# An expert stage whose rows are gathered and transposed once for two experts

## The chip, the cores and the metric

One core of a Trainium2 chip runs the whole kernel. The metric is the device time in microseconds, the median of the runs.

## The reference

One encoder layer over 512 tokens of width 2048: a mixer (two kinds of attention, gated and added to the residual) gives h, and a mixture of experts is added to it. What matters here is the second half:

```
hn = rms_norm(h, norm2_g)                       # h * r[token] * g[column]
group = argmax(hn @ w_rg + b_rg); top 2 of its 8 experts by hn @ w_re + b_re
weight = p_group * softmax(top 2)
for each expert e of 32, its tokens as rows:
    y = (silu(rows @ w_gate[e]) * (rows @ w_up[e])) @ w_down[e] * weight
    out[token] = h[token] + sum of its two y
```

silu(a) is a * sigmoid(a). Gate and up are 2048 x 512, down is 512 x 2048, float32: 12 MB an expert. There are 1024 pairs of token and expert.

## The kernel before, in words

The first half (to about 1256 us) computes h in float32 out of products of high and low parts, writes h also to a DRAM copy, h_dram, and sums the squares for the root-mean-square factor r of each token. A routing part on VectorE then makes tables with a column for each item of work and a row for each of an item's slots: `idx_x` (the token in the slot, out of bounds if it is empty), and `tab` with three fields, token, weight and r (lines 983 to 985).

An item is one expert with at most 64 tokens (SLOTS). With these inputs there are 32 items. Each engine loops over pairs of items, an even and an odd one, and the engines keep in step by semaphores alone. For an item:

- POOL gathers the rows of h_dram into `xg`, 64 x 2048, by one indirect DMA (L528 for the first, L537 in the loop). It first copies the item's column of indices (L533) and waits until TensorE has transposed the rows before. Empty slots move no row.
- ScalarE multiplies `xg` by r of each slot (`rows_scaled`, L848).
- TensorE transposes it in 16 pieces (`x_transpose`, L1612) into PSUM banks 2 and 3. VectorE copies them, times g, to `xT` (`x_copy`, L1228).
- TensorE multiplies `xT` with gate into bank 0 and with up into bank 1, 128 matmuls in four groups (L1637), one for each quarter of the weights. Half f of the columns goes to partitions 64 f and on.
- ScalarE makes the sigmoid of bank 0 (`sg`, L856), VectorE two products (`t1`, `hs`, L1258 and L1259), TensorE transposes `hs` (L1650), VectorE copies it (`hT`, L1263), TensorE multiplies by down in four groups (L1663).
- ScalarE (`y_hi`, L861) and VectorE (`y_lo`, L1275) scale by the weight and split the result into two parts. Even and odd item use different halves of the partitions. VectorE makes `place`, which has a one where the slot's token is (L1271).
- TensorE adds both items of the pair before to their tokens by `combine` (L1622), two of its eight steps after each group of the even item's gate and up, into banks 2, 3 (even steps) and 6, 7 (odd ones). VectorE adds each to `h` (`add_parts`, L1237).

The order on TensorE is written by hand: the transposes for the next item stand between the up matmuls and the down matmuls; in the even item behind the transposes of hs and a wait for the seventh add, in the odd one ahead of them.

SP issues every load of weights (`item_loads`, L446), quarters of 1 MB, in the order of use. Gate has two buffers, up and down have one, all in quarters: up and gate of the next items are loaded into a quarter as soon as a group of L1637 has used it (L403, L399), down as soon as a group of L1663 has (L406). The four buffers are filled before the first item begins, and SP then waits for its first group. Behind the last loads SP waits for the adds and writes `h` out.

Two more lines stand in the rows: L1551 transposes h for the router in pieces of 128 x 128, and L134 is a wait.

Of the kernel before, what the change touches and what calls it, by code (L numbers as in the profile page):

```python
# [27 lines left out]
F32 = mybir.dt.float32  # L28
F32R = mybir.dt.float32r
U32 = mybir.dt.uint32  # L30
# [38 lines left out]
ITEMS = EXPERTS + XTRA + 1  # L69
# [59 lines left out]
def build(nc, x, norm1_g, w_in, q_norm_a, k_norm_a, sink_a, q_norm_b, k_norm_b, rpb_pad, w_up_a, w_up_b,  # L129
# [4 lines left out]
    with ctx:  # L134
# [19 lines left out]
        xg = sb("xg", [SLOTS, D], F32, R0 + 32 * K)  # L154
        xT = sb("xT", [P, KT, SLOTS], F32, R0 + 40 * K)

        y_hi = [sb(f"y_hi{f}", [P, D // 2], F32R, (R0 + 44 * K, R3 + 32 * K)[f]) for f in range(2)]
        y_lo = [sb(f"y_lo{f}", [P, D // 2], F32R, (R0 + 48 * K, R4 + 1536)[f]) for f in range(2)]
        place = [sb(f"place{f}", [P, S], F32R, (R0 + 56 * K, R3 + 36 * K)[f]) for f in range(2)]
        sg = sb("sg", [P, F // 2], F32, R0 + 52 * K)  # L160
        t1 = sb("t1", [P, F // 2], F32, R0 + 53 * K)
        hs = sb("hs", [P, F // 2], F32, R0 + 54 * K)
        hT = sb("hT", [P, 2, P], F32, R0 + 55 * K)
        token = sb("token", [P, S], F32, R0 + 62 * K)
        tab = sb("tab", [P, 3, ITEMS], F32, R0 + 60 * K)
        idx_x = sb("idx_x", [SLOTS, ITEMS], U32, R0 + 61 * K)
        cur_x = sb("cur_x", [SLOTS, 1], U32, R0 + 61 * K + 256)
        cur = sb("cur", [P, 2], F32, R0 + 61 * K + 288)
# [68 lines left out]
        for name, shape in (("L", [P, NT, LOG]), ("gm", [P, 4]), ("gd", [P, 4, 4]), ("eg", [P, 4, 4]),  # L237
# [46 lines left out]
        (s_gu, s_dn, s_gath, s_xs, s_xt2, s_xTc, s_sgm, s_hs, s_hst, s_hTc, s_yhi, s_ylo, s_comb, s_added, s_nreg) = (  # L284
            sem(n) for n in ("s_gu", "s_dn", "s_gath", "s_xs", "s_xt2", "s_xTc", "s_sgm", "s_hs", "s_hst", "s_hTc", "s_yhi",
# [198 lines left out]
        def _(pool):  # L484
# [35 lines left out]
            items = pool.value_load(nitem[0:1, 0:1], min_val=EXPERTS, max_val=EXPERTS + XTRA)  # L520
# [9 lines left out]
            with pool.Fori(0, items) as i:  # L530

                pool.wait_ge(s_gath, i * 16 + 16)
                nc.gpsimd.tensor_copy(cur_x[:], idx_x[:, ds(i + 1, 1)]).then_inc(s_pool, 1)  # L533
                pool.wait_ge(s_pool, i + 2)
                pool.wait_ge(s_xt2, i + 1)
                settle(pool, s_pool_passed)
                gp.indirect_dma_start(xg[:], None, h_d, bass.IndirectOffsetOnAxis(ap=cur_x[:, 0:1], axis=0),  # L537
                                      bounds_check=S - 1, oob_is_err=False).then_inc(s_gath, 16)
# [21 lines left out]
        def _(act):  # L560
# [304 lines left out]
        def routing(dve, own, V):  # L865
# [117 lines left out]
            own.do(ts(idx_x[:], tab_ps[0:SLOTS, 0, :], 2.0 * S, None, ALU.add))  # L983
# [11 lines left out]
        def _(dve):  # L995
# [228 lines left out]
            g2b = bc(g2m[:], SLOTS)  # L1224
# [25 lines left out]
            with dve.Fori(0, pairs) as p:  # L1250
                own.loop(p, 0, 4)
                for odd in range(2):
                    i = p * 2 + odd
                    if not odd:
                        add_parts(p, range(6))

                    dve.wait_ge(s_sgm, i + 1)
                    own.do(V.tensor_tensor(t1[:], sg[:], PS[:, 0, 0:F // 2], ALU.mult))  # L1258
                    V.tensor_tensor(hs[:], t1[:], PS[:, 1, 0:F // 2], ALU.mult).then_inc(s_hs, 1)  # L1259
# [6 lines left out]
                    x_copy(i + 1)  # L1266

                    own.do(V.tensor_copy(cur[:], tab[:, 0:2, ds(i, 1)].rearrange("p c o -> p (c o)")))
                    for f in range(2):
                        q = slice(SLOTS * (f ^ odd), SLOTS * (f ^ odd) + SLOTS)  # L1270
                        V.tensor_scalar(place[f][q, :], token[q, :], cur[q, 0:1], None, ALU.is_equal)  # L1271
                    dve.wait_ge(s_yhi, i + 1)
                    for f in range(2):
                        q = slice(SLOTS * (f ^ odd), SLOTS * (f ^ odd) + SLOTS)
                        last = V.scalar_tensor_tensor(out=y_lo[f][q, :], in0=PS[q, 4:6, :].rearrange("p a b -> p (a b)"),  # L1275
                                                      scalar=cur[q, 1:2], in1=y_hi[f][q, :].bitcast(F32),
# [6 lines left out]
        def _(pe):  # L1283
# [457 lines left out]
```

## Time and profile before

| | us |
|---|---|
| median of 3 runs | 2326.51 |
| lowest and highest | 2323.01, 2326.81 |
| span of the profiled execution, first to last instruction | 2323.9 |
| expert stage in it, from the first gate matmul (1302.9) to the end | 1021.0 |
| busy in the span: TensorE, VectorE, ScalarE, GpSimd | 2165.1, 851.9, 650.2, 67.4 |

The page gives the profiled execution by its span; a time of the device for the same execution is not in it. The median of the runs is 2.6 us above this span. Busy TensorE means that a matmul is under way, not that it is at its peak. DMA busy share is that of the core's 16 DMA engines. The granted clock is 1.0 at TensorE's 2.4 GHz and 0.5 at 1.2 GHz.

### The profile page before, as it was taken

The page shows a single profiled execution, that of the slowest core. Times are in us where ns is not written, and L with a number is a line of the kernel's source. Part 1 is how long each engine was busy: PE and PEld are TensorE (multiplying, and loading weights), DVE is VectorE, ACT ScalarE, POOL GpSimd, SP SyncE. Part 2 cuts the span into 40 slices and gives each one's busy share as a digit, 9 for nine tenths or more (in the row PEclk, how much of TensorE's full clock was granted, in tenths as well). Part 3 has the DMA queues.
Part 4 walks back from the last instruction along what each step waited for, and adds up shares of the span by engine and source line. Part 5 has one row for each costly group of instructions (what it writes and reads, how often), then busy time and mean ns, then how long its engine had stood idle before and what let it go on. Part 6 is the DMA issues. An engine that isn't in the chain of part 4 may idle for free.

```text
span 2323.9 us, 31259 instructions
## 1 busy us (share of the span) xinstructions
PE 2165.1 (93%) x12178; PEld 1583.7 (68%) x12178; DVE 851.9 (37%) x1131; ACT 650.2 (28%) x816; POOL 67.4 (3%) x114
## 2 busy tenths in 40 slices
PE   5999999999999999999997699989988989888887
PEld 4888888888888888888886455555555555555554
DVE  4555454544222222224223433333333233333324
ACT  4446455453222222223322122212122112121121
POOL 1000000010000000000000000000000000000000
PEclk9999999999999999999998799999999999999998
DMA  5422222322333333336544599999999999999994
GB/s 178 124 82 77 86 88 76 95 78 86 95 99 96 94 99 97 92 99 195 198 147 162 195 410 408 407 415 411 408 407 399 405 410 414 405 397 410 415 388 179
DMA packets 264062, 541.99 MB, mean 233 GB/s; under 512 B 24856, under 2 KB 200152, under 8 KB 212696
## 3 DMA queue, kind: packets, MB, share of 16 engines
q1 hardware_dynamic: 260776, 532.57, 61.6%
q0 software_dynamic: 3248, 8.90, 1.4%
q8 instruction: 25, 0.41, 0.1%
q14 instruction: 13, 0.11, 0.0%
HBM read 541.93 MB, written 11.55 MB: 238 GB/s over the span
## 4 chain that ended last, share of the span: by engine, by line
PE 76%; DMA 15%; DVE 4%; issue 2%; ACT 1%; ACTq 0%; SPq 0%; DVEq 0%; POOL 0%; POOLq 0%
DMA wd_s<-in_w_down 14%; PE PS L1307 13%; PE PS L1309 13%; PE PS L1308 13%; PE PS L1637 10%; PE PS L1663 7%; PE PS L1622 5%; PE PS L1324 3%; PE PS L1326 3%; PE PS L1325 3%; PE PS L1612 2%; PE PS L1380 1%; DVE h L1237 1%; DVE y_lo L1275 1%; ACT y_hi L861 1%
## 5 line engine op out<-in xcount | busy, mean ns | idle before, releaser
L1019 DVE TENSOR_TENSOR w_lo<-w_raw,w_hi 128x1024 fp32r<-128x1024 f32 x200 | 245.0, 1225 | 673.0 <-ACT w_hi L585 673.0
L1307 PE MATMUL PS<-x_hi,w_hi 128*128 128x512 f32 x1088 | 431.2, 396 | 2.4 <-DVE x_lo L1012 2.4
L1309 PE MATMUL PS<-x_hi,w_lo 128*128 128x512 f32 x1088 | 424.6, 390 | 0.0
L1308 PE MATMUL PS<-x_lo,w_hi 128*128 128x512 f32 x1088 | 424.3, 390 | 0.0
L585 ACT ACTIVATE w_hi<-w_raw 128x1024 fp32r<-128x1024 f32 x200 | 211.8, 1059 | 703.6 <-PE PS L1309 574.9
L1637 PE MATMUL PS<-wu_s,xT 128*64 128x256 f32 x2048 | 312.4, 381 | 0.0
L1663 PE MATMUL PS<-wd_s,hT 128*64 128x512 f32 x1024 | 245.8, 631 | 33.5 <-DMA wd_s<-in_w_down 25.2
L1307 PEld LDWEIGHTS PS<-x_hi,w_hi 128*128 128x128 f32 x1088 | 204.6, 188 | 46.7 <-issue 3.0
L1308 PEld LDWEIGHTS PS<-x_lo,w_hi 128*128 128x128 f32 x1088 | 204.8, 188 | 43.5 <-issue 2.4
L1309 PEld LDWEIGHTS PS<-x_hi,w_lo 128*128 128x128 f32 x1088 | 204.6, 188 | 43.5
L1237 DVE TENSOR_TENSOR h<-h,PS 128x1024 f32<-128x1024 f32 x136 | 161.3, 1217 | 136.2 <-PE PS L1622 135.8
L1637 PEld LDWEIGHTS PS<-wu_s,xT 128*64 128x64 f32 x2048 | 153.9, 138 | 69.8 <-issue 2.6
L1663 PEld LDWEIGHTS PS<-wd_s,hT 128*64 128x64 f32 x1024 | 72.6, 142 | 178.8 <-issue 126.1
L1637 PE MATMUL PS<-wg_odd,xT 128*64 128x256 f32 x1024 | 157.4, 381 | 27.9 <-DMA wu_s<-in_w_up 27.9
L1275 DVE SCALAR_TENSOR_TENSOR y_lo<-PS,cur,y_hi 64x1024 fp32r<-64x1024 f32 x64 | 82.1, 1283 | 274.0 <-ACT y_hi L861 273.5
L861 ACT ACTIVATE y_hi<-PS,tab 64x1024 fp32r<-64x1024 f32 x64 | 71.0, 1110 | 382.8 <-PE PS L1663 382.4
L1637 PE MATMUL PS<-wg_s,xT 128*64 128x256 f32 x1024 | 160.2, 392 | 4.6 <-DMA wu_s<-in_w_up 3.0
L856 ACT ACTIVATE sg<-PS 128x256 f32<-128x256 f32 x32 | 12.3, 384 | 422.6 <-PE PS L1637 422.6
L1637 PEld LDWEIGHTS PS<-wg_odd,xT 128*64 128x64 f32 x1024 | 76.4, 137 | 74.2 <-issue 47.5
L1622 PE MATMUL PS<-y_hi,place 128*128 128x512 f32 x272 | 93.1, 424 | 24.0 <-DVE y_lo L1275 23.5
L1637 PEld LDWEIGHTS PS<-wg_s,xT 128*64 128x64 f32 x1024 | 69.9, 139 | 64.4 <-issue 25.0
L1324 PE MATMUL PS<-w_hi,m_hi 128*128 128x512 f32 x256 | 101.4, 396 | 2.8 <-DVE h L1200 2.8
(222 smaller groups left out, 2314.5 us busy)
## 6 DMA issues: line engine op xcount, KB each, us to landing
wu_s<-in_w_up SPq DMA_DIRECT2D x128, 1024.0 KB, 25.6
wd_s<-in_w_down SPq DMA_DIRECT2D x128, 1024.0 KB, 25.2
w_raw<-in_w_in SPq DMA_DIRECT2D x136, 512.0 KB, 3.8
wg_s<-in_w_gate SPq DMA_DIRECT2D x64, 1024.0 KB, 26.7
wg_odd<-in_w_gate SPq DMA_DIRECT2D x64, 1024.0 KB, 28.5
w_raw<-in_w_out SPq DMA_DIRECT2D x32, 512.0 KB, 3.9
w_raw<-in_w_up_a SPq DMA_DIRECT2D x16, 512.0 KB, 3.9
w_raw<-in_w_up_b SPq DMA_DIRECT2D x16, 512.0 KB, 3.9
```

The source lines that it names most:

```text
L585: act_fn(w_hi[:, b, :], w_raw[:, r, :], ACT.Copy).then_inc(s_whi, 1)
L861: last = act_fn(y_hi[f][q, :], PS[q, 4:6, :].rearrange("p a b -> p (a b)"), ACT.Copy, scale=tab[q, 1, ds(i, 1)])
L1019: V.tensor_tensor(w_lo[:, b, :], w_raw[:, r, :], w_hi[:, b, :].bitcast(F32), ALU.subtract).then_inc(s_wlo, 1)
L1237: V.tensor_tensor(hv, hv, PS[:, bank:bank + 2, :], ALU.add).then_inc(s_added, 1)
L1275: last = V.scalar_tensor_tensor(out=y_lo[f][q, :], in0=PS[q, 4:6, :].rearrange("p a b -> p (a b)"), scalar=cur[q, 1:2], in1=y_hi[f][q, :]. ...
L1307: mm(PS[:, bank, :], wh[:, k, :], rhs_hi[:, k0 + k, :], start=(start and k == 0), stop=False)
L1308: mm(PS[:, bank, :], wh[:, k, :], rhs_lo[:, k0 + k, :], start=False, stop=False)
L1309: last = mm(PS[:, bank, :], wl[:, k, :], rhs_hi[:, k0 + k, :], start=False, stop=(stop and k == 7))
L1324: mm(o, a_hi, b_hi, start=start, stop=False)
L1622: last = mm(PS[:, bank + f, :], place[f][:, t * P:t * P + P], y[f][:, m * S:m * S + S], start=(y is y_hi), stop=(y is y_lo))
L1637: last = mm(PS[SLOTS * f:SLOTS * f + SLOTS, bank, 0:F // 2], xT[:, k, :], w[:, k, f * (F // 2):(f + 1) * (F // 2)], start=(k == 0), stop=( ...
L1663: last = mm(PS[q:q + SLOTS, 4 + m, :], hT[:, cc, SLOTS * j:SLOTS * j + SLOTS], wd_s[:, c, f * (D // 2) + m * S:f * (D // 2) + m * S + S], ...
```

## The change

Rows are gathered once for a pair: `xg` has 128 partitions, 64 for each item, `idx_x` holds a column of indices for each pair, and POOL, x_transpose and x_copy go once a pair. The transposes are of 128 x 128 and fill banks 2, 3, 6 and 7, and x_copy takes two instructions. The transposes for the next pair stand in the odd item alone, at their former place there, behind a wait for all eight adds of the pair. The factor r is no longer applied to `xg`: sigmoid gets it as a scale, and the two products multiply by it. `cur`, the item's three fields, is copied ahead of them.

```diff
-ITEMS = EXPERTS + XTRA + 1
+ITEMS = EXPERTS + XTRA + 2
+PAIRS = ITEMS // 2
-        xg = sb("xg", [SLOTS, D], F32, R0 + 32 * K)
-        xT = sb("xT", [P, KT, SLOTS], F32, R0 + 40 * K)
+        xg = sb("xg", [P, D], F32, R0 + 32 * K)
+        xT = sb("xT", [P, KT, P], F32, R0 + 40 * K)
...
-        idx_x = sb("idx_x", [SLOTS, ITEMS], U32, R0 + 61 * K)
-        cur_x = sb("cur_x", [SLOTS, 1], U32, R0 + 61 * K + 256)
-        cur = sb("cur", [P, 2], F32, R0 + 61 * K + 288)
+        idx_x = sb("idx_x", [P, PAIRS], U32, R0 + 61 * K)
+        cur_x = sb("cur_x", [P, 1], U32, R0 + 61 * K + 256)
+        cur = sb("cur", [P, 2, 3], F32, R0 + 61 * K + 288)
...
@@ POOL @@
-            with pool.Fori(0, items) as i:
-                pool.wait_ge(s_gath, i * 16 + 16)
-                nc.gpsimd.tensor_copy(cur_x[:], idx_x[:, ds(i + 1, 1)]).then_inc(s_pool, 1)
-                pool.wait_ge(s_pool, i + 2)
-                pool.wait_ge(s_xt2, i + 1)
+            with pool.Fori(0, pairs) as p:
+                pool.wait_ge(s_gath, p * 16 + 16)
+                nc.gpsimd.tensor_copy(cur_x[:], idx_x[:, ds(p + 1, 1)]).then_inc(s_pool, 1)
+                pool.wait_ge(s_pool, p + 2)
+                pool.wait_ge(s_xt2, p + 1)
...
@@ ScalarE @@
-            def rows_scaled(i):
-                act.wait_ge(s_gath, i * 16 + 16)
-                act_fn(xg[:], xg[:], ACT.Copy, scale=tab[0:SLOTS, 2, ds(i, 1)]).then_inc(s_xs, 1)
-            rows_scaled(0)
...
-                    rows_scaled(i + 1)
                     act.wait_ge(s_gu, i * 4 + 4)
-                    act_fn(sg[:], PS[:, 0, 0:F // 2], ACT.Sigmoid).then_inc(s_sgm, 1)
+                    act_fn(hs[:], PS[:, 0, 0:F // 2], ACT.Sigmoid, scale=tab[:, 2, ds(i, 1)]).then_inc(s_sgm, 1)
...
@@ VectorE @@
-            own.do(ts(idx_x[:], tab_ps[0:SLOTS, 0, :], 2.0 * S, None, ALU.add))
+            by_pair = tab_ps[:, 0, :].rearrange("q (i o) -> q i o", o=2)
+            for o in range(2):
+                own.link(ts(idx_x[SLOTS * o:SLOTS * o + SLOTS, :], by_pair[SLOTS * o:SLOTS * o + SLOTS, :, o], 2.0 * S, None, ALU.add))
...
-            def x_copy(i):
-                dve.wait_ge(s_xt2, i + 1)
-                V.tensor_tensor(xT[:], PS[:, 2:4, :].rearrange("p a (k s) -> p (a k) s", s=SLOTS), g2b,
-                                ALU.mult).then_inc(s_xTc, 1)
+            def x_copy(p):
+                dve.wait_ge(s_xt2, p + 1)
+                for half, bank in enumerate((2, 6)):
+                    last = V.tensor_tensor(xT[:, 8 * half:8 * half + 8, :],
+                                           PS[:, bank:bank + 2, :].rearrange("p a (k s) -> p (a k) s", s=P),
+                                           g2b[:, 8 * half:8 * half + 8, :], ALU.mult)
+                last.then_inc(s_xTc, 1)
...
+                    own.do(V.tensor_copy(cur[:, odd, :], tab[:, :, ds(i, 1)].rearrange("p c o -> p (c o)")))
                     if not odd:
                         add_parts(p, range(6))
                     dve.wait_ge(s_sgm, i + 1)
-                    own.do(V.tensor_tensor(t1[:], sg[:], PS[:, 0, 0:F // 2], ALU.mult))
-                    V.tensor_tensor(hs[:], t1[:], PS[:, 1, 0:F // 2], ALU.mult).then_inc(s_hs, 1)
+                    own.do(V.scalar_tensor_tensor(out=hs[:], in0=PS[:, 0, 0:F // 2], scalar=cur[:, odd, 2:3], in1=hs[:],
+                                                  op0=ALU.mult, op1=ALU.mult))
+                    V.scalar_tensor_tensor(out=hs[:], in0=PS[:, 1, 0:F // 2], scalar=cur[:, odd, 2:3], in1=hs[:],
+                                           op0=ALU.mult, op1=ALU.mult).then_inc(s_hs, 1)
...
-                    x_copy(i + 1)
-                    own.do(V.tensor_copy(cur[:], tab[:, 0:2, ds(i, 1)].rearrange("p c o -> p (c o)")))
+                    if odd:
+                        x_copy(p + 1)
...
@@ TensorE @@
-            def x_transpose(i):
-                pe.wait_ge(s_xs, i + 1)
+            def x_transpose(p):
+                pe.wait_ge(s_gath, p * 16 + 16)
...
-                    o = PS[:, 2 + k // 8, (k % 8) * SLOTS:(k % 8) * SLOTS + SLOTS]
-                    last = nc.tensor.transpose(o, v[:, k, :], mats[0:SLOTS, 0, 0:SLOTS])
+                    o = PS[:, (2, 3, 6, 7)[k // 4], (k % 4) * P:(k % 4) * P + P]
+                    last = nc.tensor.transpose(o, v[:, k, :], ident)
...
-                pe.wait_ge(s_xTc, i + 1)
+                if not odd:
+                    pe.wait_ge(s_xTc, p + 1)
...
-                                last = mm(PS[SLOTS * f:SLOTS * f + SLOTS, bank, 0:F // 2], xT[:, k, :],
+                                last = mm(PS[SLOTS * f:SLOTS * f + SLOTS, bank, 0:F // 2], xT[:, k, SLOTS * odd:SLOTS * odd + SLOTS],
...
                 if odd:
-                    pe.wait_ge(s_added, p * 8 + 9)
-                    x_transpose(i + 1)
+                    pe.wait_ge(s_added, p * 8 + 10)
+                    x_transpose(p + 1)
                 pe.wait_ge(s_hs, i + 1)
...
-                if not odd:
-                    pe.wait_ge(s_added, p * 8 + 9)
-                    x_transpose(i + 1)
                 pe.wait_ge(s_hTc, i + 1)
```

## Rows read from the trace of the kernel before

**Rows 1.** The page's strip of 40 slices of 58 us: what the core's DMA moved
```profile
...
GB/s 178 124 82 77 86 88 76 95 78 86 95 99 96 94 99 97 92 99 195 198 147 162 195 410 408 407 415 411 408 407 399 405 410 414 405 397 410 415 388 179
...
```

**Rows 2.** Table by stretch: busy us (instructions), granted clock, DMA busy share, GB/s
```profile
...
1306.00:1308.00 2.00, 2.00 (x16) 1.23 (x14) 0.00 (x0) 1.14 (x1) 0.18 (x1) 0.65 0.02 8
1332.00:1334.00 2.00, 2.00 (x12) 0.72 (x10) 0.87 (x2) 0.00 (x0) 0.16 (x1) 1.00 0.81 238
1500.00:1700.00 200.00, 183.59 (x1243) 106.58 (x1242) 69.24 (x85) 37.52 (x32) 7.96 (x14) 0.97 1.01 409
...
```

**Rows 3.** Chain of waits, expert stage: start us, us, what
```profile
...
1302.92 5.88 PE PS L1637 x32
...
1310.83 3.60 PE PS L1637 x32
...
1364.86 1.29 DVE y_lo L1275
...
1422.42 1.29 DVE y_lo L1275
...
1543.01 1.29 DVE y_lo L1275
...
2211.89 28.77 DMA wd_s<-in_w_down
...
2246.35 1.29 DVE y_lo L1275
...
```

**Rows 4.** DMA traffic in 12 us: 1896 to 1908, 1884 to 1896, 1782 to 1794
```profile
...
DMA packets 696, 5.08 MB, mean 423 GB/s; under 512 B 76, under 2 KB 76, under 8 KB 76
...
DMA packets 711, 4.74 MB, mean 395 GB/s; under 512 B 132, under 2 KB 132, under 8 KB 132
...
q0 software_dynamic: 80, 0.16, 4.5%
...
GB/s 437 382 437 437 437 437 410 410 410 410 410 437 410 437 382 218 191 218 164 300 137 300 246 273 218 273 191 410 355 410 437 410 437 410 410 437 437 437 437 437
DMA packets 612, 4.34 MB, mean 362 GB/s; under 512 B 82, under 2 KB 82, under 8 KB 82
...
q0 software_dynamic: 80, 0.43, 14.6%
...
```

**Rows 5.** Timeline of the head: start us, us, engine, instruction [idle before <-releaser]
```profile
...
1293.02 1.01 POOL L528 DMA_INDIRECT xg<-h_dram,cur_x  x1 [0.85 <-POOL cur_x L526]
...
1297.24 2.00 ACT L848 ACTIVATE xg<-xg,tab 64x2048 f32<-64x2048 f32 x1 [22.12 <-DMA xg<-h_dram,cur_x]
...
1299.34 2.01 PE L1612 MATMUL PS<-mats,xg 64*128 64x64 f32 x16 [8.83 <-ACT xg L848]
1301.46 1.23 DVE L1228 TENSOR_TENSOR xT<-PS,g2m 128x1024 f32<-128x1024 f32 x1 [4.17 <-PE PS L1612]
...
```

**Rows 6.** Timeline of TensorE: transposes of line 1551
```profile
...
1257.31 1.09 PE L1551 MATMUL PS<-mats,h 128*128 128x128 f32 x8 [2.65 <-DVE h L1200]
...
1263.01 1.09 PE L1551 MATMUL PS<-mats,h 128*128 128x128 f32 x4
...
```

**Rows 7.** Timeline of the last pair of items
```profile
...
2254.62 2.35 DVE L1237 TENSOR_TENSOR h<-h,PS 128x1024 f32<-128x1024 f32 x2 [3.29 <-PE PS L1622]
...
2267.13 0.42 DVE L1263 COPY hT<-PS 128x256 f32<-128x256 f32 x1
...
2267.45 1.94 PE L1612 MATMUL PS<-mats,xg 64*128 64x64 f32 x16 [0.44 <-DVE h L1237]
...
2269.33 7.09 PE L1663 MATMUL PS<-wd_s,hT 128*64 128x512 f32 x32
...
2292.60 0.42 DVE L1263 COPY hT<-PS 128x256 f32<-128x256 f32 x1 [1.04 <-PE PS L1650]
...
2293.08 0.20 PEld L1663 LDWEIGHTS PS<-wd_s,hT 128*64 128x64 f32 x4 [0.71 <-DVE hT L1263]
...
```

**Rows 8.** Transfers of wd_s issued from 2240 to 2246 us
```profile
...
DMA to landing us min/median/max: 27.2/27.5/27.7
...
```

More of the change, by code:

```diff
@@ L153, in build @@
         wd_s = sb("wd_s", [P, 4, D], F32, R0)
-        xg = sb("xg", [SLOTS, D], F32, R0 + 32 * K)
-        xT = sb("xT", [P, KT, SLOTS], F32, R0 + 40 * K)
[L157 to L163, printed above, removed]
+        xg = sb("xg", [P, D], F32, R0 + 32 * K)
+        xT = sb("xT", [P, KT, P], F32, R0 + 40 * K)
+        y_hi = [sb(f"y_hi{f}", [P, D // 2], F32R, (R0 + 48 * K, R3 + 32 * K)[f]) for f in range(2)]
+        y_lo = [sb(f"y_lo{f}", [P, D // 2], F32R, (R0 + 52 * K, R4 + 1536)[f]) for f in range(2)]
+        place = [sb(f"place{f}", [P, S], F32R, (R0 + 58 * K, R3 + 36 * K)[f]) for f in range(2)]
+        hs = sb("hs", [P, F // 2], F32, R0 + 56 * K)
+        hT = sb("hT", [P, 2, P], F32, R0 + 57 * K)
         token = sb("token", [P, S], F32, R0 + 62 * K)
         tab = sb("tab", [P, 3, ITEMS], F32, R0 + 60 * K)
-        idx_x = sb("idx_x", [SLOTS, ITEMS], U32, R0 + 61 * K)
-        cur_x = sb("cur_x", [SLOTS, 1], U32, R0 + 61 * K + 256)
-        cur = sb("cur", [P, 2], F32, R0 + 61 * K + 288)
+        idx_x = sb("idx_x", [P, PAIRS], U32, R0 + 61 * K)
+        cur_x = sb("cur_x", [P, 1], U32, R0 + 61 * K + 256)
+        cur = sb("cur", [P, 2, 3], F32, R0 + 61 * K + 288)
         eid = sb("eid", [P, XTRA], I32, R0 + 61 * K + 320)
@@ L283, in build @@
         s_wd = [sem(f"s_wd{c}") for c in range(4)]
-        (s_gu, s_dn, s_gath, s_xs, s_xt2, s_xTc, s_sgm, s_hs, s_hst, s_hTc, s_yhi, s_ylo, s_comb, s_added, s_nreg) = (
-            sem(n) for n in ("s_gu", "s_dn", "s_gath", "s_xs", "s_xt2", "s_xTc", "s_sgm", "s_hs", "s_hst", "s_hTc", "s_yhi",
+        (s_gu, s_dn, s_gath, s_xt2, s_xTc, s_sgm, s_hs, s_hst, s_hTc, s_yhi, s_ylo, s_comb, s_added, s_nreg) = (
+            sem(n) for n in ("s_gu", "s_dn", "s_gath", "s_xt2", "s_xTc", "s_sgm", "s_hs", "s_hst", "s_hTc", "s_yhi",
                              "s_ylo", "s_comb", "s_added", "s_nreg"))
@@ L519, in _ @@
             pool.wait_ge(s_r1, 1)
-            items = pool.value_load(nitem[0:1, 0:1], min_val=EXPERTS, max_val=EXPERTS + XTRA)
+            pairs = pool.value_load(nitem[0:1, 2:3], min_val=EXPERTS // 2, max_val=(EXPERTS + XTRA) // 2)
             pool.wait_ge(s_hd, 16 * NT)
@@ L1223, in _ @@
             pairs = dve.value_load(nitem[0:1, 2:3], min_val=EXPERTS // 2, max_val=(EXPERTS + XTRA) // 2)
-            g2b = bc(g2m[:], SLOTS)
-            def x_copy(i):
-                dve.wait_ge(s_xt2, i + 1)
-                V.tensor_tensor(xT[:], PS[:, 2:4, :].rearrange("p a (k s) -> p (a k) s", s=SLOTS), g2b,
-                                ALU.mult).then_inc(s_xTc, 1)
+            g2b = bc(g2m[:], P)
+            def x_copy(p):
[5 more added lines that the diff above has]
+                last.then_inc(s_xTc, 1)
             def add_parts(p, parts):
@@ L1265, in _ @@
                         add_parts(p, (7,))
-                    x_copy(i + 1)
-                    own.do(V.tensor_copy(cur[:], tab[:, 0:2, ds(i, 1)].rearrange("p c o -> p (c o)")))
+                    if odd:
+                        x_copy(p + 1)
                     for f in range(2):
                         q = slice(SLOTS * (f ^ odd), SLOTS * (f ^ odd) + SLOTS)
-                        V.tensor_scalar(place[f][q, :], token[q, :], cur[q, 0:1], None, ALU.is_equal)
+                        V.tensor_scalar(place[f][q, :], token[q, :], cur[q, odd, 0:1], None, ALU.is_equal)
                     dve.wait_ge(s_yhi, i + 1)
@@ L1275, in _ @@
                         last = V.scalar_tensor_tensor(out=y_lo[f][q, :], in0=PS[q, 4:6, :].rearrange("p a b -> p (a b)"),
-                                                      scalar=cur[q, 1:2], in1=y_hi[f][q, :].bitcast(F32),
+                                                      scalar=cur[q, odd, 1:2], in1=y_hi[f][q, :].bitcast(F32),
                                                       op0=ALU.mult, op1=ALU.subtract)
```

## The prediction

> **What bounds the kernel now.** I read the 40-slice strip of the page first. From the 24th slice on, where the experts run, the core moves about 408 GB/s in every slice but the last two, against 77 to 198 before [rows 1]. The table by stretch says how full that is: from 1500 to 1700 us the DMA engines are 1.01 busy at 409 GB/s while TensorE is busy 183.59 of 200 us [rows 2]. So the expert stage is a stream of weights, 32 experts of 12 MB. The chain of waits agrees and adds a history [rows 3]. The low halves of the result (y_lo) of even items follow each other by 1422.42 - 1364.86 = 57.6 us while TensorE still works on weights that came early; from 1543.01 to 2246.35 there are 11 pairs of items, 63.9 us each, and each such pair has a wait on a transfer of wd_s in the chain, such as the 28.77 us from 2211.89. A pair of items that TensorE could do in 57.6 us takes the 63.9 us that its weights need. Engine time removed in the middle of the stage therefore buys nothing. The change can act in three places: on the stream itself, before the stream is full, and after the last weights.
>
> **The stream.** What disturbs it are the gathers of xg. In 12 us without one, 5.08 MB move (423 GB/s). In 12 us around a gather that brings 0.16 MB (19 rows of 8 KB) it is 4.74 MB, around one that brings 0.43 MB (53 rows) 4.34 MB, gathered bytes included [rows 4]. So these losses come on top of the gathered bytes. The first loses 0.34 MB = 0.80 us of stream, the second 0.74 MB = 1.75 us. A straight line through both gives 0.0118 MB, 0.028 us, for each row and a remainder of 0.12 MB, 0.28 us, for a gather as such. Both gathers have 80 packets, 64 slots and 16 more, so an empty slot is part of that remainder. The change makes 17 gathers of 128 slots out of 33 of 64, with the same 1024 rows. Per-row loss stays. If slots make the remainder, it stays too; if the gather as such does, half of it goes. Bounds: 0 and 0.28 us. I take 0.15, the middle, since nothing in the rows separates them. Some 15 of the 16 dropped gathers lie in the full stream: 15 x 0.15 = **-2.2 us** (0 to -4.2). The gather of a pair may land later than now; it is issued right after the transposes of the pair before, so some 50 of the 63.9 us cover it.
>
> **Removed, and worth nothing by itself.** Scaling xg on ScalarE, 2.00 us 33 times [rows 5], runs while TensorE is in its matmuls, except for the first one. Every second x_transpose, x_copy and index copy of POOL goes; the tile sg becomes hs, and the factor moves into the sigmoid's scale and the two products, which keep their count and size (0.42 us each). The copy of cur moves ahead of the products; 0.16 us, behind which only adds wait whose matmuls come later. POOL's wait for a gather, then for the transpose, now happens once a pair; nobody stands behind it. x_transpose in the odd item now waits for all eight adds of the pair, made a whole item earlier. SP's queue issues what it did, in the same order.
>
> **Before the stream is full: the head.** Now: the gather is issued at 1293.02, ScalarE starts at 1297.24, the transposes at 1299.34, the copy at 1301.46, the matmuls at 1302.92 [rows 5]. After:
> - two index operations for one, 50 columns for 49 in the routing tables: +0.2.
> - the gather of 64 + 64 slots: 4.2 us from issue to use for 64 slots. Between +0 (all latency) and +4.2 (all proportional); +1.2, nearer to latency, since the dent that 53 rows make in the stream spans only 12 or 13 slices of 0.3 us, 3.8 us [rows 4].
> - no scaling: from 1297.24 to 1299.34, -2.1.
> - 16 transposes of 128 x 128 instead of 64 x 128. This is a low-clock stretch (clock 0.65 from 1306 to 1308, and the first group of 32 matmuls of L1637 takes 5.88 us against 3.60 later) [rows 2, 3]. Transposes of 128 x 128 in L1551 took 1.09 us for 8 before the clock fell and 1.09 for 4 after it [rows 6]. So 16 of them take about 2.1 us at the high level and 3.7 at the low one; now 2.01. I take +1.7 (0 to +1.7).
> - two copies of 128 x 1024: two such operations run in 2.35 us [rows 7], one in 1.23: +1.1.
>
> Sum +2.1. The first group starts later but spends less of itself at the low clock, up to 1.1 us back if the clock rises when it does now; I count +1.6 (-1 to +5). The transfers wait for that group, so the stream starts 1.6 later. Against it stands the first even item: its x_transpose (1.94 us between the last gate and up matmul and the first of the down matmuls) is gone, so wd_s comes free relatively earlier. Now there is a hole: 238 GB/s from 1332 to 1334 [rows 2], 0.9 us of stream. It closes: -0.9. **Head: +0.7.**
>
> **After the last weights: the tail.** From 2246.35 on the chain is TensorE's without a wait on weights. In the last even item hT's copy starts at 2267.13 but the down matmuls at 2269.33, behind the transposes; in the odd item, where nothing stands between, they start 0.48 after that copy (2292.60 to 2293.08) [rows 7]. So the even item's down matmuls start at 2267.6: -1.7. The weights just allow it: wd_s took up to 27.7 us to land [rows 8], so the last quarter, issued before 2245, is there by 2272.7, and would be wanted 5.3 us after the start, at 2272.9. In the odd item the transposes of 128 slots stand between gate/up and the down matmuls; at the high clock 16 take 2.1 us by L1551 against 1.94 to 2.01 now: +0.1 (up to +1.7 at the low level's price). hs is ready under them. The doubled x_copy stands ahead of y_lo on VectorE, 1.1 us longer, but y_lo has to wait for ScalarE anyway, which waits for down matmuls of 7.09 us [rows 7]. **Tail: -1.6.**
>
> **Sum.** -2.2 + 0.7 - 1.6 = -3.1 us on a span of 2323.9. The median of the runs shown, 2326.5, is 2.6 above that span; with the same distance I forecast 2323.4, 0.13% less. About 0.2%, 4.7 us, is what a measurement of this kernel can tell from no change, so the forecast is: no difference that counts.
>
> **Rivals.**
> A, faster: the loss belongs to the gather, not to its rows, because the packets of one gather run in one batch on each DMA engine. Then 15 gathers less save up to their mean loss, (0.80 + 1.75)/2 = 1.3 us each: -19, or about 2306 with the other terms. Against it: 53 rows cost more than twice what 19 do [rows 4]. For it: no row shows a gather of 128 slots.
> The Trainium skill, page DMA: Bandwidth & Descriptors, section Anatomy of one DMA, speaks for more: about 2.0 us fixed for each DMA from GpSimd. If that were stream time, 15 gathers less would give -30 us. The trace disagrees: the smallest gather shown costs 0.80 us in all, so most of any fixed part is latency beside a busy stream.
>
> B, slower: the slots that hold tokens fall on fewer DMA engines. They are the first ones of each 64. If 128 slots are dealt so that those land on eight engines, each of these carries 64 rows more than an even share. One of sixteen engines moves 423/16 = 26.4 GB/s, so a row costs its engine 0.0082 MB/26.4 = 0.31 us for its bytes and 16 x 0.028 = 0.45 beyond them. 64 x 0.76 = 49 us, and the stream ends with its slowest engine: about 2372, less by what the rows are uneven already. It decides in the middle of the stage, as soon as rates between gathers fall below 423.
> The Trainium skill, same page, section The descriptor swizzle, says engines 0 to 7 write partitions 0 to 63 and 8 to 15 the others, four partitions each in turn; by that the first 32 slots of both halves spread over all sixteen, and B would not happen. No row here names an engine.
>
> C, slower at both ends: the first gather's time is proportional (+3 beyond my term), the clock stays low a little longer (+2), transposes cost 3.7 in the tail too (+1.6), the fixed gather cost stays (+2.2). About 2332.
>
> **Chances.** Forecast case 0.70, A 0.15, B 0.06, C 0.09. The forecast case's own range is 2318 to 2329; some of it, and A, lie more than 0.2% below 2326.5: 0.30 faster. B and most of C: 0.13 slower. The rest, 0.57, within. The range for 8 in 10 takes the forecast case whole, the near part of A and half of C: 2313 to 2332.
>
> **What would show it.** In the profile after: between 1500 and 2200 the pair of items again at 63.5 to 64 us and the DMA engines at 1.0; TensorE's idle before wd_s larger by about 1.7 us a pair; a dent of 1.5 to 2.9 us of stream for each of 16 gathers, in place of two of half that; first matmul of L1637's line at about 1305 instead of 1302.92; from the last even y_lo to the end about 1.6 us less than 2323.9 - 2246.35 = 77.6. A pair under 63 us would make A right; a rate between gathers under 420 GB/s would make B right; a first matmul after 1307, C. The forecast is wrong if the median leaves 2313 to 2332.

## The result, and the profile after

| | before | after |
|---|---|---|
| median of 4 runs each, us | 2325.8 (2323.01 to 2326.81) | 2291.02 (2288.81 to 2292.28) |
| ratio, 95% interval | | 0.9853 [0.9842, 0.9865] |
| profiled execution, us | span 2323.9 | time 2290.01, span 2288.1 |

The change takes 34.8 us away. I had forecast 3.1, with a range that ended at 2313 below. The mechanism that pays is one that I had priced and then assumed to stay.

The strip of the page comes first again (40 slices, now of 57 us), then the table by stretch, with columns as in [rows 2].

```profile
...
GB/s 179 121 89 79 78 89 86 81 87 83 94 99 95 98 95 97 96 96 195 197 120 92 208 392 421 421 422 421 422 422 421 422 422 421 422 422 422 421 420 208
...
```

```profile
...
1328.00:1330.00 2.00, 1.23 (x6) 0.67 (x4) 0.84 (x2) 1.07 (x2) 0.00 (x0) 1.00 0.89 291
1334.00:1336.00 2.00, 2.00 (x13) 0.59 (x10) 0.00 (x0) 0.00 (x0) 0.00 (x0) 1.00 0.71 176
1500.00:1700.00 200.00, 181.47 (x1260) 103.89 (x1258) 71.62 (x88) 23.99 (x25) 3.61 (x6) 1.00 1.01 422
...
```

Where [rows 1] has 397 to 415 GB/s from the 24th slice to the 38th, the 25th to the 39th now hold 420 to 422. The DMA engines are 1.01 busy in both tables, at 409 GB/s in [rows 2] and at 422 here: they were as busy and moved less. TensorE is busy 181.47 of the 200 us (183.59 before) although the stage goes faster: it now makes 16 transposes of xg for a pair instead of 32.

The chain of waits of the expert stage (start us, us, what) gives the landmarks that [rows 3] gave.

```profile
...
1303.68 6.58 PE PS L1638 x32
...
1366.10 1.29 DVE y_lo L1275
...
1423.44 1.29 DVE y_lo L1275
...
1539.67 1.29 DVE y_lo L1275
...
2212.41 1.29 DVE y_lo L1275
...
2230.96 1.28 ACT L848
2235.28 7.09 PE PS L1661 x32
...
2258.94 7.11 PE PS L1661 x32
...
```

Set against [rows 3], three distances account for the whole. The first even y_lo stands at 1366.10, 1.24 later than 1364.86. From there to the last even y_lo it is 2212.41 - 1366.10 = 846.3 us against 881.5: 35.2 less. From that y_lo to the end it is 2288.1 - 2212.41 = 75.7 against 77.6: 1.9 less. 1.2 - 35.2 - 1.9 = -35.9, the difference of the spans (35.8) but for rounding. The 11 pairs from 1539.67 to 2212.41 take 61.2 us each; they took 63.9. The pair that TensorE paces is what it was: 1423.44 - 1366.10 = 57.3 against 57.6. So the head and the tail came out near the forecast, and the stream, where I counted 2.2 us, gave all the rest.

What a gather costs the stream is read from the DMA traffic. First the 12 us from 1710 to 1722, around a gather of 0.74 MB, 90 rows; then the traffic of the same 11 pairs in both kernels: before from 1543.01 to 2246.35, after from 1539.67 to 2212.41.

```profile
...
DMA packets 736, 5.06 MB, mean 422 GB/s; under 512 B 118, under 2 KB 118, under 8 KB 118
...
q0 software_dynamic: 144, 0.74, 15.0%
...
```

```profile
...
GB/s 420 403 417 410 422 402 398 421 397 421 397 421 390 392 410 422 388 400 423 404 422 399 422 397 394 421 423 394 381 422 381 423 405 422 397 398 422 401 392 401
DMA packets 40222, 286.13 MB, mean 407 GB/s; under 512 B 5296, under 2 KB 5296, under 8 KB 5296
...
q0 software_dynamic: 1760, 6.06, 3.2%
...
```

```profile
...
GB/s 422 421 422 420 421 424 420 422 422 421 421 421 422 421 421 422 424 421 421 421 422 421 421 421 422 422 422 421 422 421 421 422 421 422 422 422 421 421 421 420
DMA packets 39751, 283.64 MB, mean 422 GB/s; under 512 B 5130, under 2 KB 5130, under 8 KB 5130
...
q0 software_dynamic: 1584, 5.70, 2.1%
...
```

In [rows 4], 53 rows left 4.34 MB of the 5.08 that 12 us can hold. Now 90 rows leave 5.06. Over the 11 pairs of before, 286.13 MB would take 678.0 us at 422 GB/s; they took 703.3, so 25.3 us were lost beyond the bytes, for 6.06 MB, 740 rows. After, 283.64 MB need 672.1 of 672.7 us: 0.6 us lost, for 696 rows. The rows are still moved. Only their surcharge is gone. This quantity, **the time beyond the bytes at 422 GB/s**, is the measure of all that follows. The 422 is itself the rate of after, to three digits, so a loss of 1 or 2 us in 700 is not told from none. Counted from the first even y_lo on, with the three pairs ahead of the 11 (73.00 and 73.15 MB), before loses 30.5 us and after 0.8: that is 29.6 of the 35.2 us. The other 5.5 are 2.34 MB that the change moves outside this stretch and before moves within it.

### The profile page after: what moved, and what is told of

It is laid out like the page before. It is cut to its first block, busy times and chain, and to the rows that moved or that the text cites. A ratio compares the mean times of both kernels' runs of the same rounds, so it can differ in the third digit from the quotient of the medians.

```text
span 2288.1 us, 30507 instructions
## 1 busy us (share of the span) xinstructions
PE 2121.8 (93%) x11922; PEld 1547.4 (68%) x11922; DVE 853.2 (37%) x1133; ACT 566.3 (25%) x767; POOL 50.3 (2%) x82
## 4 chain that ended last, share of the span: by engine, by line
PE 78%; DMA 13%; DVE 4%; issue 2%; ACT 2%; ACTq 0%; SPq 0%; DVEq 0%; POOL 0%; POOLq 0%
PE PS L1307 13%; PE PS L1309 13%; PE PS L1308 13%; PE PS L1638 12%; DMA wd_s<-in_w_down 8%; PE PS L1661 7%; PE PS L1622 5%; DMA wu_s<-in_w_up 4%; PE PS L1324 3%; PE PS L1326 3%; PE PS L1325 3%; PE PS L1380 1%; ACT L848 1%; PE PS L1558 1%; DVE y_lo L1275 1%
## 5 line engine op out<-in xcount | busy, mean ns | idle before, releaser
L1661 PE MATMUL PS<-wd_s,hT 128*64 128x512 f32 x1024 | 230.8, 600 | 41.8 <-DVE hT L1263 23.5
```

The lines of the kernel that those rows point to most:

```text
L1661: last = mm(PS[q:q + SLOTS, 4 + m, :], hT[:, cc, SLOTS * j:SLOTS * j + SLOTS], wd_s[:, c, f * (D // 2) + m * S:f * (D // 2) + m * S + S], ...
```

## The experiments

The diff changes several things about a gather at once: how many there are, how many slots each has, and on which partitions of xg they land. The kernels pull these apart. e1 to e4 ran on one chip beside 19 runs of before (2324.6 us), e5 to e8 on one with 7 (2325.71), e9 and e10 with 7 (2326.23).

**e1: 33 gathers of 128 slots, the upper 64 always empty.** From before: xg, xT's source, idx_x and cur_x get 128 partitions. All rows still land on partitions 0 to 63.

```diff
-        xg = sb("xg", [SLOTS, D], F32, R0 + 32 * K)
+        xg = sb("xg", [P, D], F32, R0 + 32 * K)
...
-            own.do(ts(idx_x[:], tab_ps[0:SLOTS, 0, :], 2.0 * S, None, ALU.add))
+            own.link(ts(idx_x[0:SLOTS, :], tab_ps[0:SLOTS, 0, :], 2.0 * S, None, ALU.add))
+            own.do(ts(idx_x[SLOTS:P, :], tab_ps[SLOTS:P, 0, :], 0.0, 2.0 * S, ALU.mult, ALU.add))
```

> The kernel before, with one thing changed: xg and its indices have 128 partitions and the upper 64 slots are always empty, so the 33 gathers, their rows and everything else stay. Theory 1 (a row costs stream time beyond its bytes because the gather is written for 64 partitions): the stream runs at 421 to 423 GB/s through every gather, a pair of items takes 61.2 us instead of 63.9, and the time is about 2325.8 - 32 x 1.05 = 2292; if the rows now fall on eight of the sixteen DMA engines, up to 20 us more than that. Theory 2 (the loss is one of each gather, and the change gained because it has 17 for 33): 33 dents of about 1 us as before, 2326. Theory 3 (scaling xg in place disturbs the stream): also 2326.

**e3: the same 33 gathers of 128 slots, but items take the halves in turn.** Even items fill slots 0 to 63, odd ones 64 to 127, and the other half is empty. Scaling and transposes follow the half.

```diff
+            for o in range(2):
+                q = slice(SLOTS * o, SLOTS * o + SLOTS)
+                own.link(ts(idx_x[q, o::2], tab_ps[q, 0, o::2], 2.0 * S, None, ALU.add))
+                own.link(ts(idx_x[q, 1 - o::2], tab_ps[q, 0, 1 - o::2], 0.0, 2.0 * S, ALU.mult, ALU.add))
...
-                act_fn(xg[:], xg[:], ACT.Copy, scale=tab[0:SLOTS, 2, ds(i, 1)]).then_inc(s_xs, 1)
+                act_fn(xg[q, :], xg[q, :], ACT.Copy, scale=tab[q, 2, ds(i, 1)]).then_inc(s_xs, 1)
```

> The kernel before, with 128 slots in each of the 33 gathers, of which even items fill the lower 64 and odd items the upper 64; scaling and transposes work on that half. Same rows, same number of gathers. Theory 1: no dents, 421 to 423 GB/s all through, 2292, and 2291 to 2294 whatever the lower-half kernel gives, since both groups of engines get rows. Theory 2: 2326. Theory 3: 2326.

Measured: e3 2292.68 us, ratio 0.9864 [0.9847, 0.9880]; e1 2315.26, 0.9956 [0.9939, 0.9972]. Traffic of the 11 pairs of e3 (1537.81 to 2214.49):

```profile
...
DMA packets 41465, 284.94 MB, mean 421 GB/s; under 512 B 6686, under 2 KB 6686, under 8 KB 6686
...
q0 software_dynamic: 3168, 6.06, 2.4%
...
```

284.94 MB need 675.2 of 676.7 us: 1.5 us lost in 22 gathers, with the same 740 rows for which before lost 25.3. **e3 keeps before's number of gathers, its scaling, its transposes and its copies, and has the gain of the change**, 31.9 us against its own before where the change has 34.8; the intervals of 0.9864 and 0.9853 overlap. What pays is neither fewer gathers nor less work on any engine; it is that the gather spans 128 partitions instead of 64. The rows themselves still land on 64 partitions, the lower or the upper ones by turns; the other 64 slots of each gather are empty. Doubling the slots cost nothing that can be seen: 3168 packets on the gather's queue instead of 1760.

e1 has the same wide gather and 22.6 us more. Its strip, and the 12 us from 1943 to 1955 around a gather of 0.32 MB (39 rows):

```profile
...
GB/s 172 125 88 78 81 93 76 88 87 82 99 92 100 96 95 100 93 97 196 191 143 143 201 407 421 421 421 421 421 421 409 409 408 409 402 401 406 418 382 173
...
```

```profile
...
DMA  9999999975575395699999999999999989578999
...
DMA packets 700, 4.33 MB, mean 361 GB/s; under 512 B 172, under 2 KB 172, under 8 KB 172
...
q0 software_dynamic: 144, 0.32, 8.1%
...
```

Up to about 1740 us the slices hold 421 like e3's; from there they fall to 401 to 418. In the 12 us some slices have the engines busy 3 to 7 tenths only, and 0.75 MB less goes through than the 5.08 that fit. That is what rival B described: rows that all fall on part of the engines, which fall behind by their extra bytes until the weights wait for them. B's own numbers fit. 64 of the 128 rows on such an engine are above an even share, and 64 x 0.31 us = 19.8 us of bytes; measured 22.6. The 0.45 us a row beyond the bytes that I had added to it was not there, although all rows land on the same partitions 0 to 63 as in before. The trace shows the lag itself. It keeps 16 completion marks for each weight transfer, as many as there are DMA engines. Over the transfers of up and down, the first and the last of the 16 lie 3.7 us apart in e1 (median) between 1350 and 1450 us and 19.9 us apart between 1750 and 1850; in e3 it is 2.8 and 9.4. The Trainium skill, page DMA: Bandwidth & Descriptors, section The descriptor swizzle, has engines 0 to 7 write partitions 0 to 63 of a 128-partition transfer and 8 to 15 the others; e1 and e3 agree with that by 22.6 us, though no row names an engine.

**e2: the change with two gathers of 64 partitions for each pair**, one into partitions 0 to 63, one into 64 to 127.

```diff
-                gp.indirect_dma_start(xg[:], None, h_d, bass.IndirectOffsetOnAxis(ap=cur_x[:, 0:1], axis=0),
+                gp.indirect_dma_start(xg[0:SLOTS, :], None, h_d, bass.IndirectOffsetOnAxis(ap=cur_x[:, 0:1], axis=0),
                                       bounds_check=S - 1, oob_is_err=False).then_inc(s_gath, 16)
+                gp.indirect_dma_start(xg[SLOTS:P, :], None, h_d, bass.IndirectOffsetOnAxis(ap=cur_x[:, 1:2], axis=0),
+                                      bounds_check=S - 1, oob_is_err=False).then_inc(s_gath, 16)
```

> The changed kernel, with the 128 slots of a pair filled by two gathers of 64 partitions each, one right behind the other, into the lower and the upper half of xg. Theory 1: the whole loss is back, 0.03 us a row, 2291 + 32 x 1.05 = about 2325. Theory 2, counted by gathers: about 2325 as well; counted by times at which gathers disturb the stream (16 as in the changed kernel): 2291 to 2308. Theory 3 (scaling xg in place): stays at 2291.

Measured: 2328.9 us, ratio 1.0018 [1.0008, 1.0028]. The pair takes 64.1 us. Traffic of its 11 pairs (1546.37 to 2251.23):

```profile
...
GB/s 422 422 422 374 422 422 369 422 423 421 348 423 422 409 366 424 422 367 423 422 421 351 423 421 406 351 423 422 355 421 422 423 361 421 420 410 364 422 414 420
DMA packets 40211, 285.71 MB, mean 405 GB/s; under 512 B 5337, under 2 KB 5337, under 8 KB 5337
...
```

285.71 MB need 677.0 of 704.9 us: 27.8 lost. Everything of the change is in this kernel but the width of the gather, and the gain is gone, with 0.2% more. For 696 rows 27.8 us are 0.040 us a row, more than before's 0.034; why isn't known. The slices show it by eye: 422, and 348 to 374 where a double gather stands. Using both halves of the partitions by turns doesn't help; each transfer has to span all 128.

**e4: the factor moved alone.** The scaling of xg goes, as in the change; gathers, transposes and copies stay per item.

```diff
-            rows_scaled(0)
...
-                    rows_scaled(i + 1)
...
-                    act_fn(sg[:], PS[:, 0, 0:F // 2], ACT.Sigmoid).then_inc(s_sgm, 1)
+                    act_fn(sg[:], PS[:, 0, 0:F // 2], ACT.Sigmoid, scale=tab[:, 2, ds(i, 1)]).then_inc(s_sgm, 1)
...
-                    own.do(V.tensor_tensor(t1[:], sg[:], PS[:, 0, 0:F // 2], ALU.mult))
+                    own.do(V.scalar_tensor_tensor(out=t1[:], in0=PS[:, 0, 0:F // 2], scalar=cur[:, odd, 2:3], in1=sg[:], op0=ALU.mult, op1=ALU.mult))
...
```

> The kernel before, with the root-mean-square factor moved to the sigmoid's scale and the two products, and no scaling of xg on ScalarE; items are gathered and transposed one by one as before. Theories 1 and 2: the stream keeps its dents, and only the head gets shorter by the first scaling, about 2 us; less up to 1.3 us where a table load of ScalarE comes into the chain of the last even item: 2323 to 2326. Theory 3: the dents go, about 2291.

Measured: 2328.8 us, ratio 1.0022 [1.0012, 1.0031]: 4.2 us slower, though the first group of gate and up matmuls lets its first transfer go 4.7 us earlier than before's. Table by stretch and timeline of e4:

```profile
...
1320.00:1340.00 20.00, 18.24 (x98) 9.07 (x96) 6.17 (x9) 3.97 (x4) 1.13 (x2) 0.83 0.81 293
...
```

```profile
...
1321.17 1.28 ACT L849 ACT_TABLE_LOAD   x1 [47.14 <-PE PS L1630]
...
1322.47 0.47 ACT L849 ACTIVATE sg<-PS,tab 128x256 f32<-128x256 f32 x1
...
```

And ScalarE's timeline of before, for the same even item:

```profile
...
1310.19 1.28 ACT L856 ACT_TABLE_LOAD   x1
1325.76 0.39 ACT L856 ACTIVATE sg<-PS 128x256 f32<-128x256 f32 x1 [14.29 <-PE PS L1637]
...
```

Before, the same 20 us held 363 GB/s at a clock of 1.00 and 19.56 us of TensorE; here 293 at 0.83 and 18.24. (363 - 293) x 20 / 422 = 3.3 us of stream go there. The timeline shows what stands in it: the sigmoid is preceded by a load of ScalarE's function table, 1.28 us. Before, that load followed the scaling at 1310.19 and was long done when the sigmoid's wait ended at 1325.76. With the scaling gone the sigmoid is the first activation after y_hi, the load stands behind the wait, and in the even item TensorE has nothing to do in that time. In the last even item the same load is followed by a down group of 8.69 us at low clock. Why the clock fell isn't shown: the change has the same load in its first even item, at 1327.32, and its clock stays at 1.00 from 1320 to 1340 us. 11 pairs of e4 lose 26.0 us, as before's do. Against before's trace, e4's first even y_lo is 0.4 us earlier, the way from there to the last one is 0.7 longer, and from that one to the end 1.5, in which the load is 1.28. These make 1.8 us; the rest of the 4.2 between the medians is in no trace. The time is above the 2323 to 2326 expected.

**e5 and e6: the disputed cost by itself.** In both, each item's rows are replaced by a plain transfer of the first 64 rows of h (the routing's choice of rows is left out), so the gathered bytes are the same for every item: e5 into 64 partitions, e6 into 128, each row in two halves. 33 x 64 = 2112 rows each, no index read, every slot full.

```diff
e5
+                gp.dma_start(xg[:], h_d[0:SLOTS, :]).then_inc(s_gath, 16)
e6
+                gp.dma_start(xg[:, 0:D // 2], h_d[0:SLOTS, :].rearrange("s (o c) -> (s o) c", o=2)).then_inc(s_gath, 16)
```

> The kernel before, with each of the 33 gathers replaced by a plain transfer from the same queue of GpSimd, rows 0 to 63 of h into the 64 partitions of xg (so the right rows are no longer fetched, and 64 rows come instead of 32 on average). 1088 more rows are 8.9 MB, 21 us of stream. If any transfer into 64 partitions loses 0.032 us a row: 2325 + 21 + 1088 x 0.032 = 2381. If only indirect ones do: 2292 + 21 = 2313.

> The same plain transfer of 64 rows, but as 128 half rows of 4 KB into 128 partitions (the other half of xg stays zero, so the values are not the rows). Same bytes as in the plain transfer into 64 partitions. If the 64-partition form is what costs: no loss, 421 GB/s, 2292 + 21 = 2313. If the bytes of GpSimd's queue cost: 2381 as well.

**e9 and e10: the same two transfers from ScalarE's queue**, so POOL issues nothing.

```diff
e9
+                    act.wait_ge(s_xt2, i + 2)
+                    act.dma_start(xg[:], h_d[0:SLOTS, :]).then_inc(s_gath, 16)
e10
+                    act.dma_start(xg[:, 0:D // 2], h_d[0:SLOTS, :].rearrange("s (o c) -> (s o) c", o=2)).then_inc(s_gath, 16)
```

> As the plain transfer into 64 partitions, but issued from ScalarE's queue instead of GpSimd's (GpSimd does nothing in the expert stage; the 64 rows are again rows 0 to 63, not the gathered ones). If the 64-partition form costs the stream whichever queue issues it: dents as with GpSimd's, about 0.027 us a row, 2355 to 2362. If it takes GpSimd's queue: 421 GB/s throughout, about 2302.

> The same 64 rows from ScalarE's queue as 128 half rows into 128 partitions. Both theories: 421 GB/s throughout, 2300 to 2304. It is the reference for the other one: the difference of the two is what the form costs on this queue.

Measured: e5 2359.58 us (1.0150 [1.0133, 1.0167]), e6 2302.02 (0.9897 [0.9881, 0.9914]); e9 2359.94 (1.0148 [1.0131, 1.0165]), e10 2302.85 (0.9906 [0.9889, 0.9922]). Traffic of 11 pairs: e5 from 1552.77 to 2278.51, e6 from 1541.86 to 2226.29, e9 from 1554.05 to 2279.80.

```profile
...
DMA packets 39794, 288.51 MB, mean 398 GB/s; under 512 B 4578, under 2 KB 4578, under 8 KB 4578
...
q0 software_dynamic: 1760, 11.54, 6.2%
...
```

```profile
...
DMA packets 41190, 288.42 MB, mean 421 GB/s; under 512 B 4577, under 2 KB 4577, under 8 KB 7393
...
q0 software_dynamic: 3168, 11.54, 4.2%
...
```

```profile
...
DMA packets 39762, 288.26 MB, mean 397 GB/s; under 512 B 4576, under 2 KB 4576, under 8 KB 4576
...
q10 hardware_dynamic: 1760, 11.54, 6.3%
...
```

The same bytes, the same stream, one shape against the other: e5 is 57.6 us above e6, e9 57.1 above e10. Over 2112 rows that is **0.027 us a row**, the 0.028 of [rows 4], now without an index, without an empty slot, and on either queue. By traffic, e5 loses 725.7 - 683.7 = 42.1 us for 1408 rows (0.030), e6 684.4 - 683.5 = 1.0. Neither the indirection nor POOL's queue is needed for it. e6 also halves the pieces, from 8 to 4 KB; e3, whose rows are whole, shows that this isn't what saves. Nor are the rows of a 64-partition transfer dealt to some of the engines only: in e5 the 16 completion marks of a weight transfer stay 1.8 to 2.2 us apart (medians by 100 us) from 1350 us to the end, where e1's drift to 20.

The level of e5 was missed: 2359.6, where 2381 was expected for a loss with any 64-partition transfer and 2313 for none. It shares 11 of these 21 us with e6; the other 10 are the price of a row, 0.027 us, where 0.032 had been counted. e6 came out 11 us below what was expected, 9.3 above e3 where 1088 more rows are 8.9 MB, 21 us. Two readings say where the rest went. Over their 11 pairs e6 moved 276.88 MB of weights (the other queue's share of its 288.42) and e3 278.87: for the same items, e3's transfers ran 2 MB further ahead, 4.7 us; its first three pairs take 57.5 us each, TensorE's pace, where e6's third already takes 60.7. And this is the end of the stream, slices of 2.0 us from 2210 in e3 and of 1.9 us from 2226 in e6:

```profile
...
GB/s 418 434 414 418 426 418 426 418 426 397 410 320 377 356 246 275 402 365 426 426 381 147 49 37 0 0 0 0 0 0 0 0 0 0 197 393 434 418 393 262
...
```

```profile
...
GB/s 418 423 418 418 427 423 427 423 418 418 423 418 418 427 423 412 420 435 414 414 423 418 362 69 0 0 0 0 0 0 0 0 0 0 345 414 414 414 414 207
...
```

e3's last weights arrive in slices of 246 to 426, as if the transfers waited for TensorE to free buffers; e6's arrive at full rate to their end. So once the surcharge is gone the stage isn't bound by the stream at its two ends, and added bytes are partly free there. How the 12 us divide between the two ends stays open.

**e7: the change, with the sigmoid's table loaded early.** One activation of one column, in even items, ahead of the wait for TensorE.

```diff
+                    if not odd:
+                        act_fn(es[:, 0:1], eps[:, 0:1], ACT.Sigmoid)
                     act.wait_ge(s_gu, i * 4 + 4)
```

> The changed kernel, with one small sigmoid on ScalarE ahead of its wait for the even item's gate and up, so that the table load (1.28 us, 16 times, in the chain where TensorE sets the pace) is over when the wait ends. Theory: the load is hidden by the stream in the middle, and stands in the chain in the first pairs and in the last one: 1.3 us less at the end, up to 1.3 in the head: 2288 to 2290 against 2291. Rival: the load is covered by the stream throughout: 2291.

**e8: e7, and the transposes of a pair handed on in halves**, so that the first gate and up matmuls start after 8 of the 16 transposes and one of the two copies.

```diff
                     last = nc.tensor.transpose(o, v[:, k, :], ident)
-                last.then_inc(s_xt2, 1)
+                    if k % 8 == 7:
+                        last.then_inc(s_xt2, 1)
...
-                if not odd:
-                    pe.wait_ge(s_xTc, p + 1)
                 for c in range(4):
+                    if not odd and c == 0:
+                        pe.wait_ge(s_xTc, p * 2 + 1)
...
+                            pe.wait_ge(s_xTc, p * 2 + 2)
                             pe.wait_ge(s_ylo, i + 1)
```

> As the kernel with the early table load, and the transposes and copies of xg handed on in two halves: VectorE copies the first eight while TensorE transposes the others, and the matmuls start behind the first copy. In the head that takes 1.2 us of copy and up to 1.2 of transposing out of the path to the first release of a weight buffer: 2 us less than with the early table load alone, 2286 to 2288. Rival: TensorE's clock rises later by as much, and nothing is gained.

Measured: e7 2287.48 us (0.9837 [0.9820, 0.9853]; 2288 to 2290 expected), e8 2283.1 (0.9817 [0.9801, 0.9834]). Chain of e7's last even item, then timeline of e8's head:

```profile
...
2212.03 1.29 DVE y_lo L1277
...
2230.57 0.48 ACT hs L850
...
2233.60 7.09 PE PS L1663 x32
...
```

```profile
...
1298.80 3.39 PE L1613 MATMUL PS<-mats,xg 128*128 128x128 f32 x16 [7.14 <-DMA xg<-h_dram,cur_x]
...
1300.86 2.59 DVE L1225 TENSOR_TENSOR xT<-PS,g2m 128x1024 f32<-128x1024 f32 x2 [2.22 <-PE PS L1613]
...
1302.31 0.65 PE L1640 MATMUL PS<-wg_s,xT 128*64 128x256 f32 x4
...
1306.09 0.33 SPq L402 DMA_DIRECT2D wu_s<-in_w_up  x1
...
```

In e7 the down matmuls follow y_lo by 21.6 us, against 22.9 in the change: the 1.3 us of the load. Its first even y_lo, at 1365.62, is 0.5 earlier, and from the last one to the end it takes 74.8 us instead of 75.7: 1.4, where the spans differ by 1.3. The medians, from two chips, differ by 3.5, with ratios whose intervals overlap, so they don't tell it from nothing; the 1.4 us of the traces is what is shown for the early load. In e8 the copy starts while transposes run, and the first weights' buffer is released at 1306.09, 4.3 us before the change's 1310.38; e8 is 4.4 us below e7 on the same chip, where 2 were expected. It is the fastest version, ahead of both kernels: 42.6 us below before.

## Why the prediction was wrong, step by step

**"Per-row loss stays": this step failed, and it is the whole error.** From [rows 4] I had 0.028 us of stream per row beyond its bytes, and [rows 3] show it to be real: 740 rows x 0.028 + 22 gathers x 0.28 = 26.9 us for the 11 pairs, where the traffic now shows 25.3. The size was right, and so was the law in rows for the gathers that it was taken from. But both gathers in those rows had 64 partitions, and I carried the number over to a gather of 128 as if it belonged to the row. It belongs to the form of the transfer: 25.3 us lost in 11 pairs of before, 27.8 in e2, 26.0 in e4, 42.1 in e5, all with 64 partitions, against 0.6 in the change, 1.5 in e3 and 1.0 in e6. The bounds that I gave to the unknown (0 and 0.28 us for each gather) enclosed only the remainder, and the larger term had none: below it I should have put 0. 1024 rows x 0.028 = 28.7 us, so with 0 below for it the range would have reached down to 2323.4 - 28.7 = 2294.7 before any other bound. **The -2.2 us of the stream was -35.2.**

**What was known and unused.** The engines were 1.01 busy at 409 GB/s in [rows 2], and 423 GB/s went through between gathers in [rows 4]. As busy and moving less: I now read that as engines held up within their transfers, and the form of the gather, which the diff changes from 64 to 128 partitions, could have been the cause. I gave it no term. The Trainium skill, page SBUF — State Buffer, section Door 1: The DMA port swizzle, says that partitions 0 to 63 are reached through 8 of 16 ports, so that 64 partitions are no better than 32. Its figures would halve the rate of a row that is written so, 0.019 us more for 8 KB at 422 GB/s, an estimate; the runs show 0.027 to 0.040 for transfers of 64 partitions.

But which partitions the rows reach doesn't decide. In e3 the rows of one gather land on 64 partitions too, and in e1 on the same 0 to 63 as in before; e3 loses 0.002 us a row, and e1 runs at 421 GB/s up to 1740 us. What sets the price is how many partitions the transfer spans, its empty slots included. By e1's backlog, a transfer that spans 128 leaves the lower half to a part of the engines; by e5's even marks, one that spans 64 is carried by all. So more engines than ports could meet at 64 partitions, and that would fit the runs. No row names a port or an engine: the width of the transfer is shown as the cause, the ports are argued.

**Rival A** had the right side and a wrong cause. Its sign appeared (a pair under 63 us), but e3, with as many gathers as before, has the gain, and 22 of them lose 1.5 us, 0.07 each. The 2.0 us fixed for each DMA, which the Trainium skill's page DMA: Bandwidth & Descriptors gives in its section Anatomy of one DMA, would cost e3's 22 gathers 44 us if they were time of the stream, an estimate; e3 shows 1.5, so here they are not.

**Rival B** didn't happen in the change, and happened in e1, where all rows lie in the lower half: +22.6 us, its bytes, without the surcharge. Its sign, a rate that falls in mid-stage, is how I would look for it again.

**The head: +0.7 forecast, +1.24 at the first y_lo.** Timeline of the change's head, to be set against [rows 5]:

```profile
...
1292.67 1.09 POOL L527 DMA_INDIRECT xg<-h_dram,cur_x  x1 [0.84 <-POOL cur_x L525]
...
1297.32 3.65 PE L1612 MATMUL PS<-mats,xg 128*128 128x128 f32 x16 [7.35 <-DMA xg<-h_dram,cur_x]
...
1301.09 2.35 DVE L1223 TENSOR_TENSOR xT<-PS,g2m 128x1024 f32<-128x1024 f32 x2 [4.14 <-PE PS L1612]
...
1303.68 1.12 PE L1638 MATMUL PS<-wg_s,xT 128*64 128x256 f32 x4 [2.71 <-DVE xT L1223]
...
1310.38 0.33 SPq L402 DMA_DIRECT2D wu_s<-in_w_up  x1
...
```

From issue to transposes it takes 4.65 us where the old gather took 4.22 to ScalarE's start: +0.4 instead of +1.2. The sixteen transposes take 3.65 us and the copies 2.35, both as priced. The issue itself is 0.35 earlier instead of 0.2 later. So the first matmul is 0.76 later, not 2.1; but its group then takes 6.58 us against 5.88, at a granted clock of 0.55 against 0.62; the first transfer goes at 1310.38, 1.5 after before's, where I had counted 1.6. "It closes: -0.9" was wrong. The hole moved from 1332 to 1334 us to 1328 to 1330 (291 GB/s) and 1334 to 1336 (176), and the stretch from 1320 to 1340 moves 354 GB/s against 363. In it stands the table load that e4 shows, here at 1327.32. e7, with the load early, moves 373 GB/s there, but 170 against 186 in the 20 us before, so how much of the hole is the load's stays open. I had put the scaling under "Removed, and worth nothing by itself"; it was what kept that load ahead of the wait.

**The tail: -1.6 forecast, -1.9 measured, for another reason.** "The even item's down matmuls start at 2267.6: -1.7": they follow y_lo by 22.87 us against 22.98. The transposes did leave, and the load of 1.28 us at 2230.96, the longer sigmoid (0.47 against 0.39) and products (0.48 against 0.42 each) came in their place. What was gained is the last down group: 7.11 us at a clock of 1.00 against 8.81 at 0.81. The traces don't show why the clock is high there now; before had 0.83 in its row from 2290 to 2300 us, which I hadn't used.

## What to carry to other kernels

When a full stream of wide transfers shares the DMA engines with small ones, let the small ones span all 128 partitions too, with empty slots if need be; and fill both halves, in one transfer or by turns, since rows that all lie in one half cost 22.6 us here (e1). A loss fitted per row or per transfer holds only for the form in which it was measured: if the change alters that form, the whole loss is unknown and not only its remainder. Compare the rate at full busy share with the rate between disturbances before deciding what the disturbance belongs to.

## What the runs showed of the hardware that I had not expected

- A transfer that spans 64 partitions costs a full stream 0.027 (e5 against e6) to 0.040 us (e2) for each 8 KB row beyond its bytes (0.0194 us at 422 GB/s), indirect or plain, from POOL's or ScalarE's queue, on partitions 0 to 63 alone or by turns with 64 to 127. If it spans 128, the surcharge is about 0.002 us a row (e3: 1.5 us for 740), even where the rows fill only 64 of them.
- An empty slot costs the stream nothing that can be seen: e3 has 1408 more of them in its 11 pairs than before has.
- A busy share of 1.01 stands beside 398 (e9), 409 (before) and 422 GB/s (after). It doesn't tell whether the stream is at its rate.
- Removing an activation can expose a table load of 1.28 us: in e4 and in the change the load stands directly ahead of the sigmoid, behind the sigmoid's wait. An activation of one column ahead of the wait takes it off the chain (e7).
